# A seven-product projection: column sets reordered, pooling spread over two sets, weight sums in two slots, and the first block's sums moved from GpSimd to VectorE

## The reference

```python
h = rms_norm(x, norm_pre) * (1.0 + scale) + shift
u = h @ w_in                       # 1024 x 3720
q, k, v, f_logit, z_rwkv, p_pool, g = split(u)
y = concat[fox_attention(q, k, v, f_logit), rwkv7(z_rwkv), multiscale_pool(p_pool)] * silu(g)
x = x + gate * rms_norm(y @ w_out, norm_post)
```

## Time and profile before

| what | us |
|---|---|
| median of 3 runs (lowest, highest) | 3746.25 (3742.59, 3747.57) |
| the profiled execution | 3759.72 |
| its span, first to last instruction | 3758.0 |
| end of the projection's last product | 1525.88 |
| first product of the projection | 175.40 |
| `single` of the second block pair starts | 571.80 |
| ... of the third, of the fourth | 890.45, 1209.50 |

### The profile page before, as it was taken

How to read it: one execution, slowest core, us unless ns; L and a number is a source line. 1 busy time by engine, 2 the same in 40 slices (tenths; PEclk the granted TensorE clock), 3 DMA queues, 4 the chain that set the end, 5 groups by cost and what they waited for, 6 DMA issues and landing times. The chain is left out here.

```text
span 3758.0 us, 90231 instructions
## 1 busy us (share of the span) xinstructions
PE 3356.4 (89%) x31941; PEld 2300.8 (61%) x31941; DVE 2344.9 (62%) x4080; ACT 2051.6 (55%) x3774; POOL 1918.5 (51%) x2320
## 2 busy tenths in 40 slices
PE   6466898999899899599999789999999999989998
PEld 6322495487369349488888656656656656654454
DVE  4545452353245233578777199988989989974544
ACT  1334553454354342467776457777777767763333
POOL 1776433131332310235554269889889888871222
PEclk9688899999999999789998589999999999999999
DMA  8256552444345344323221130211202202214555
GB/s 315 73 202 213 206 178 99 155 153 144 121 149 184 113 151 158 84 67 84 70 64 43 27 84 8 55 33 30 57 15 48 56 10 53 57 49 162 192 179 184
DMA packets 237659, 406.35 MB, mean 108 GB/s; under 512 B 86542, under 2 KB 188645, under 8 KB 222085
## 3 DMA queue, kind: packets, MB, share of 16 engines
q1 hardware_dynamic: 236747, 400.56, 33.6%
q0 software_dynamic: 480, 0.14, 0.1%
HBM read 278.05 MB, written 122.59 MB: 107 GB/s over the span
## 5 line engine op out<-in xcount | busy, mean ns | idle before, releaser
L2456 ACT ACTIVATE p<-psc,xb,sc 128x512 f32<-128x512 f32 (+3 forms) x1152 | 848.3, 743 | 320.5 <-PE psc L2547 307.7
L2434 POOL TENSOR_TENSOR plo<-p 128x512 f16<-128x512 f32 (+2 forms) x864 | 903.6, 1073 | 74.3 <-ACT p L2456 72.7
L2603 DVE TENSOR_REDUCE mx<-pm 128x1 f32<-128x512 f32 (+3 forms) x1201 | 730.4, 636 | 94.0 <-PE pm L2478 80.1
L579 PE MATMUL bank<-h,ring 128*128 128x512 f16 x2688 | 625.4, 393 | 49.3 <-ACT p L719 22.7
L2526 PE MATMUL po<-v,p 128*128 128x129 f16 x4224 | 513.3, 220 | 21.4 <-POOL plo L2434 18.4
L579 PEld LDWEIGHTS bank<-h,ring 128*128 128x128 f16 x2688 | 270.9, 101 | 419.0 <-issue 95.8
L2528 PE MATMUL po<-v,plo 128*128 128x65 f16 x4224 | 483.8, 192 | 4.5 <-issue 4.5
L2526 PEld LDWEIGHTS po<-v,p 128*128 128x128 bf16 x4224 | 388.9, 97 | 124.2 <-POOL plo L2434 28.3
L584 PE MATMUL bank<-ring,h 128*128 128x128 f16 x8064 | 457.2, 219 | 2.3 <-ACT c L726 2.3
L584 PEld LDWEIGHTS bank<-ring,h 128*128 128x128 f16 x8064 | 453.7, 98 | 4.3 <-issue 2.9
L2478 PE MATMUL pm<-ka,qa 128*128 128x512 f16 (+3 forms) x1201 | 439.9, 369 | 3.3 <-DVE mx L2603 3.0
(11 more groups left out here) (385 smaller groups left out, 5777.9 us busy)
## 6 DMA issues: line engine op xcount, KB each, us to landing
ring<-scratch_ws SPq DMA_DIRECT2D x54, 1792.0 KB, 7.9
scratch_ws<-h SPq DMA_DIRECT2D x12, 1792.0 KB, 6.7
scratch_z<-stage SPq DMA_DIRECT2D x72, 256.0 KB, 7.8
y<-scratch_y SPq DMA_DIRECT2D x35, 512.0 KB
g<-scratch_g SPq DMA_DIRECT2D x35, 512.0 KB
xr<-in_x SPq DMA_DIRECT2D x34, 512.0 KB, 6.2
scratch_qk<-stage SPq DMA_DIRECT2D x64, 256.0 KB, 2.6
scratch_g<-stage SPq DMA_DIRECT2D x64, 256.0 KB, 7.9
```

Source lines behind the costliest of these rows:

```text
L579: t = nc.tensor.matmul(bank[b][:], m.ring[:, slot, l, bo, k, :], hh[:, side, r, ao, k, :], start=fresh and first, stop=last, skip_group_ch ...
L2434: nc.gpsimd.tensor_tensor(plo[:, k % NP, 0:w], p32[:, k % NP, 0:w], hi[:, 0:w], ALU.subtract)\
L2456: nc.scalar.activation(p32[:, k % NP, 0:w], psc[k % 2][:, 0:w], ACT.Exp, bias=xb[:, u, b, x // 4:x // 4 + 1], scale=m.sc[:, 0:1]).then_inc ...
L2603: nc.vector.tensor_reduce(mx[:, s, t, q:q + 1], pm[g][:, 0, 0:w], AX.X, ALU.max).then_inc(pm_d.sem, 1)
```

## The change

1. `m.kinds` becomes `m.sets`: a set is a pair of slices with a name for each side. The order is now g, g, g, g, v, v, qk, (z7, z0), qk, (z8, z1), qk, (z2, z3), qk, (z4, z5). Each pooling slice is paired with an ordinary z slice. Each raw set is fetched by two DMAs of 128 columns, where there was one of 256.
2. The first block pair's units: the row scaling of groups 1 to 3 moves from DVE in `prepare` (line 280, six instructions) to POOL in `project`; all four A parts come from ACT (two instructions), the sums S1 to S4 are on DVE (`first_sums`), and units use four slots (two of `h7`, two in `c`). The products of `single` for a group of 128 rows follow the transposes of the next group.
3. POOL does, beside the six scalings, the sums of the single slice and of set 0, and their rounding, which was ACT's. Set 1 is made in the loop.
4. Sets 1 to 13 are made at steps 1, 6, 13, 17, 21 and from 25 on every fourth step (`MADE`). `wt` has a second slot, in `xt`. ACT's and DVE's shares are done in two parts each, two steps apart (`weights_high_a`, `_b`, `weights_low_a`, `_b`). Sets 0 to 3 are made in place in the ring, where before sets 0 and 1 were.
5. The units for the second block pair begin at step 60, ten steps a group; those for the third and fourth stay at 51 and twelve.
6. p1 is gone: the first product is copied into u1, which is summed in place. The table `it16` is made in `prepare`.

```diff
-        m.kinds = (("qk", 0), ("z", 7), ("qk", 1), ("z", 0), ("qk", 2), ("z", 2), ("qk", 3), ("z", 4),
-                   ("g", 0), ("g", 1), ("g", 2), ("g", 3), ("v", 0), ("v", 1))
+        pairs = (("g", 0, 1), ("g", 2, 3), ("g", 4, 5), ("g", 6, 7), ("v", 0, 1), ("v", 2, 3), ("qk", 0, 1), ("z", 7, 0),
+                 ("qk", 2, 3), ("z", 8, 1), ("qk", 4, 5), ("z", 2, 3), ("qk", 6, 7), ("z", 4, 5))
...
+        wts = [m.wt, m.xt[:].rearrange("p s d -> p (s d)").rearrange("p (o k c) -> p o k c", o=4, k=4)]
...
-            q = 2 + 2 * (at[1] - 1) + at[2] // 4
-            return q if q < NSET else None
+        MADE = (-1, 0, 1, 6, 13, 17, 21, *range(25, 54, 4))
+        DIRECT = 4
+        def production(g, after):
+            r = g - after
+            return MADE.index(r) - 1 if 1 <= r < SUBS and r in MADE else None
+        def turns_of(sb_):
+            return (60, 10, (0, 1, 3, 4), 2, 6) if sb_ == 0 else (51, 12, (0, 2, 4, 6), 3, 7)
...
+                def first_sums(u):
+                    x = raw_slot(u)
+                    dve.wait_ge(raw_first, u + 1)
+                    tt(x[:, S1, :], x[:, A21, :], x[:, A22, :], ALU.add).then_inc(s_first, 1)
+                    tt(x[:, S3, :], x[:, A11, :], x[:, A21, :], ALU.subtract).then_inc(s_first, 1)
+                    dve.wait_ge(s_first, 4 * u + 1)
+                    tt(x[:, S2, :], x[:, S1, :], x[:, A11, :], ALU.subtract).then_inc(s_first, 1)
+                    dve.wait_ge(s_first, 4 * u + 3)
+                    tt(x[:, S4, :], x[:, A12, :], x[:, S2, :], ALU.subtract).then_inc(s_first, 1)
...
                 for u in range(18):
                     if u < 16:
-                        raw_low(u)
-                    if u == 5:
-                        weights_low(-1)
-                    if u == 11:
-                        weights_low(0)
-                    if 1 <= u < 17:
-                        low(u - 1)
-                weights_low(1)
+                        first_sums(u)
+                    if u == 6:
+                        single_low()
+                    if u >= 2:
+                        low(u - 2)
+                    if u == 14:
+                        weights_low_a(0)
+                    if u == 15:
+                        weights_low_b(0)
...
+                    if production(g, 2) is not None:
+                        weights_high_a(production(g, 2))
+                    if production(g, 4) is not None:
+                        weights_high_b(production(g, 4))
...
+                    if production(g, 3) is not None:
+                        weights_low_a(production(g, 3))
+                    if production(g, 5) is not None:
+                        weights_low_b(production(g, 5))
...
+                x_first_scaled(1)
+                single_weights()
+                x_first_scaled(2)
+                x_first_scaled(3)
+                weight_sums(0)
+                first_high()
```

More of the change, by code:

```diff
@@ L366, in kind, with item @@
         def kind(n):
-            return m.kinds[n - 1]
+            return m.sets[n - 1][0][0]
+        def item(n, side):
+            return m.sets[n - 1][side][1]
         def tile(sb_, n, half, side):
@@ L441, in unit_at @@
-        def unit_at(at):
-            if at is None or at[0] == NSB - 1:
-                return None
-            r = ended(0, at[1], at[2]) - 1 - 51
-            if r < 0 or r % 12 not in (0, 2, 4, 6) or r // 12 > 3:
-                return None
-            return (at[0] + 1) * 16 + (r // 12) * 4 + (r % 12) // 2
+        shifts = [(0, 0, 0), (0, 1, 0)] + [(n, half, side) for n in range(1, NSET + 1) if kind(n) == "z"
+                                           for half, side in ((0, 0), (1, 0), (0, 1), (1, 1)) if not is_pool(n, side)]
@@ new lines, in single @@
+                    ts = slice(j * P, (j + 1) * P)
+                    if j == 0:
+                        if sb_ == 0:
+                            pe.wait_ge(w_lo, 1)
+                        else:
+                            pe.wait_ge(c_act, sb_ * (NSET + 2))
+                            pe.wait_ge(u1_d, sb_ * NSET)
+                            pe.wait_ge(f_out, sb_)
+                    pe.wait_ge(lo_made, sb_ * 16 + 4 * (j + 1))
+                    for half, parts in enumerate((((A11, 0), (A12, 1)), ((S1, 0), (A22, 2)))):
+                        for y, (ao, bo) in enumerate(parts):
+                            for k in range(4):
+                                for x, (l, r) in enumerate(((0, 0), (0, 1), (1, 0))):
+                                    nc.tensor.matmul(bank[half][:, ts], wz[:, l, bo, k, :], hh[:, side, r, ao, k, ts],
+                                                     start=(j == 0 and y == 0 and k == 0 and x == 0),
+                                                     stop=(y == 1 and k == 3 and x == 2), skip_group_check=True)
@@ L635, in head_means @@
                     nc.tensor.matmul(pss[:], m.headmean[:], sq[:, x % 2, :], start=True, stop=True).then_inc(ss_d, 1)
-                for u in range(16):
-                    turn(u)
+                for j in range(5):
+                    if j < 4:
+                        for k in range(4):
+                            turn(4 * j + k)
+                    if j:
+                        single(0, j - 1)
                 for g in range(NG + LAST):
@@ L903, in shifted @@
                     s = t % NC
-                    dve.wait_ge(own_d, sb_ * NZ + z_order(n, half, side) + 1)
+                    dve.wait_ge(own_d, sb_ * NZ + shifts.index((n, half, side)) + 1)
                     if z_before(sb_, n, half, side):
@@ L910, in shifted @@
                         .then_inc(ready[s], 1)
-                def z_order(n, half, side):
-                    if n == 0:
-                        return half
-                    return 2 + 4 * sum(kind(y)[0] == "z" and not is_pool(y) for y in range(1, n)) + 2 * side + half
                 def z_before(sb_, n, half, side):
                     if half == 1:
-                        return sb_ * NZ + z_order(n, 0, side) + 1
-                    if sb_ == 0:
-                        return 0
-                    return (sb_ - 1) * NZ + z_order(n, 1, side) + 1
+                        return sb_ * NZ + shifts.index((n, 0, side)) + 1
+                    return (sb_ - 1) * NZ + shifts.index((n, 1, side)) + 1 if sb_ else 0
                 def value_low(sb_, n, half, side):
@@ L1076, in pieces @@
                 def pieces(sb_, n, half, side):
-                    t, x = tile(sb_, n, half, side), qk_number(sb_, n, half, side)
+                    t, x = tile(sb_, n, half, side), nth(sb_, n, half, side)
                     s = t % NC
```

492 lines of the change are left out of this document (260 added, 232 removed).

## The result

The changed kernel takes 3706.24 us (median of 4 runs, 3698.74 to 3716.05) against 3746.91 (median of 4 runs beside it): 40.7 us less, ratio 0.9893 with a 95% interval of 0.9868 to 0.9919. The forecast was 3666, 80 us less. The time lies in the stated range (3605 to 3715) but outside the forecast's own of 3640 to 3695, and about half of the gain is missing.

What follows compares the result with a forecast made beforehand. It took POOL's and DVE's turns at SBUF, not PE, to bound weight making in the first block pair. Gains 23 + 39 + 3 + 3 + 12 = 80 us gave 3680 profiled, median 3666; own range 3640 to 3695, stated range 3605 to 3715.

Steps and rivals of the forecast that it cites:

- The start: Up to the first product: it comes at 152 instead of 175.4 us, 23 us gained (18 to 42).
- Steps 1 to 57: First block pair, where 13 weight sets are made: POOL and DVE taking turns at SBUF set the length, 212 us.
- POOL and DVE together near full: Expected sign in the first block pair's steps 1 to 57, with 200 to 220 us and clock about 0.85.
- A second slot for the sums takes away POOL's wait: Weight making, first block pair: POOL's wait for the subtraction goes, but SBUF turns remain, so the slot itself gains nothing.
- Steps 58 to 98: Rest of the first block pair: products, `pss`, transposes and 15 us of waits from units among qk and pooling tiles, 145 us.
- block pairs 2 and 3: Second and third block pairs: spread pooling gains more than units among qk sets cost, 3 us gained in each.
- Back come about 9.5. Bounds are nothing and 19: Block pairs 2 and 3: new waits, 5 us at the second qk set and 4 for units between logarithms.
- The 12.5 go: Later block pairs: pairing each pooling slice with a z slice removes the 12.5 us excess behind the pooling set.
- pair 4: Fourth block pair, which has no units: 12 us gained.
- C: Rival, chance 0.14: ACT's in-order waits behind pooling tiles twice as large, production 230 us, gain 26 us, total 3720.
- D: Rival, chance 0.07: weight sets take 25 us each, results stay in PSUM, PE stands; slower, 3767 us.
- B: Rival, chance 0.18: POOL and DVE turns cost less, steps 1 to 57 take 180 us, gain 146 us, total 3600.

Runs made afterwards that it cites:

- e4: Changed kernel with the row scaling of groups 1 to 3 back on DVE in `prepare`: 3707.36 us.
- e12: Changed kernel with e7's unit places and the start of e9 (scaling on DVE, `single` products two units later): 3655.47 us, 0.9756 of the kernel before.
- e10: Changed kernel with DVE's low-half weight subtractions replaced by one-input scalings by 1.0 (low halves wrong): 3699.32 us.
- e5: Changed kernel with the order of sets turned back, qk and z first, then g and v: 3655.40 us.
- e13: Changed kernel with only one slot for the weight sums, POOL waiting for DVE's last subtraction: 3712.60 us.
- e3: e1 with both pooling slices in one set again: 3742.29 us.
- e7: Changed kernel with the units of block pairs 2 and 3 moved 44 steps earlier, same spacing (steps 7 to 49): 3666.29 us.
- e1: Changed kernel with the units of block pairs 2 and 3 at steps 8 to 44, ten steps a group: 3687.22 us, 0.9842 of the kernel before.
- e9: Changed kernel with e5's order of sets, e4's scaling on DVE, and `single` products two units later: 3649.53 us, 0.9725 of the kernel before.
- e14: e9 with the one weight-sum slot of e13: 3647.53 us, 0.9714 of the kernel before.

## Why the prediction was half right

**The start (23 forecast, 18.9 measured).** The mechanism held: sums and subtractions stretched beside POOL, and a first scaling 7 us behind the barrier. The scalings were mis-sized, 19.6 us and not 9, 3.3 each, outside the bounds of 1.2 to 1.8 that I had drawn from a cast and from half of a 2048-element instruction; the prediction's other estimate, 1.54 us, was too low as well, since the shortest of the six took 2.83. PE's order (`single` before the next transposes) was a wait that I had not counted; the scaling back on DVE brought 3.0 us (e4, 153.5), PE's order another 6.3 (e12, 147.2).

**Steps 1 to 57 (212 forecast, 198 measured).** The turns are real: e10 shows that what DVE saves in them comes off nearly in full, and e5 that qk and pooling tiles in these steps add 39 us (the prediction's sum has 29 for qk and 28 for pooling tiles at the old order). "POOL and DVE together near full" holds as well, though POOL alone is busy only 136 of 198 us and waits 51 for raw weights: DVE works in 39 of these 51, and counted instruction by instruction at least one of the two works in 182 of the 198 us. The length fell just below the 200 to 220 that I had named, and the clock was 0.92, not 0.85. "A second slot for the sums takes away POOL's wait" was right, and that nothing is gained by it as well; that it costs 8 us (e13) was not foreseen.

**Steps 58 to 98 (145 forecast, 162 measured), block pairs 2 and 3 ("Back come about 9.5. Bounds are nothing and 19").** This is the step that failed. "The 12.5 go" is right (e3: 12.8 to 15.1), and pair 4 shows it undisturbed (14.0 against 12). But what comes back is 25.6 in pair 2 and 26.1 in pair 3 (after against e5), beyond the upper bound. I had named the very chain, unit behind pooling tiles, row norm before the square, at 5 us; it took 7.5 us in two waits (710.13 and 718.99). The 4 us for units between logarithms came about as said (3.5: two waits of 2.79, where a `pss` without units waits 1.06). Two kinds I did not count: the next group's rows scaled late (2.75) and the edge from the last z set over `single` into a g set (3.7 in place of 1.3). So the waits are 15.3 and not 9.5. And I priced waits alone, putting the clock at nothing: around five of the six waits it fell to 0.50 for 3.4 or 6.8 us, and the slower matmuls made the other 10.3 of the 25.6.

Steps 58 to 98 of the first pair are the same thing, and larger. In pair 4, without units, PE takes 124.0 us for these 41 steps and stands still for 5.9 of them (first row below). In pair 2 it is 151.3 us, or 123.8 with the units moved away (e7). In the first pair it is 161.7 us and PE stands still for 30.1: 37.7 us more than in pair 4, 24.2 of them waits and 13.5 slower matmuls, where the prediction's sum has 15. The last two rows are the longest waits. The first transposes wait for scaled rows, which I had not counted, and the first `pss` behind the pooling tiles, where ACT stands 9.8 us at a unit's rounding, took 9.8 us and not 7.

```profile
1357.50:1481.50 124.00, 118.11 (x518) 52.45 (x517) 41.50 (x78) 54.91 (x72) 43.91 (x47) 1.00 0.35 124
```

```profile
370.56 1.12 PE L665 MATMUL ptr<-ident,xt 128*128 128x128 f32 x4 [7.93 <-DVE xt L909]
...
435.00 2.07 PE L673 MATMUL pss<-sq,headmean 128*128 128x512 f32 x2 [9.77 <-ACT sq L790]
```

The account up to the last product, 35.6 us short of 80: pairs 2 and 3 30.9 (forecast +6.0, measured -24.9), the start 4.1, the first pair 2.6 (14 won in its first part, 17 lost in its second), and 2.0 back in pair 4.

**Of the rivals,** C was nearest in mechanism and size: it had 160 for the last steps, a loss of 6 in pairs 2 and 3, and 3720, though its slow production (230 us) did not come. D did not come, and B's pace of the production was not reached either.

Left open: why the one slot is worth 8 us in one order of sets and 2.5, if anything, in the other; and why the last 41 steps cost 10 us more in the first pair (161.7) than in the second and third (151).

## What to carry to other kernels

A new order of work must be priced in every stretch that repeats it: this one freed the stretch in which the weights are made, which comes once, and loaded the second half of three block pairs, in which the units had stood among light sets. Two in-order chains that each hide well (running sums, the making of h) need not hide in one another; move one of them by a constant and look, before anything else is undone. Where the engine at the end is PE, add to the waits something for the clock (here 10.3 us on 15.3 us of waits), and before you buy a second buffer, find the next thing for which the same engine will wait.

## What the runs showed of the hardware

- The scaling by a column of 1024 f32 elements in SBUF takes 2.84 us on POOL and 0.68 on DVE (4.06 for six).
- POOL starts to compute some 7 us behind the barrier that ends `prepare`, whatever comes first: IOTA at 92.29 in the kernel before (barrier 85.3), the scaling at 89.09 (81.7), the product of e4 at 92.55 (85.2). Only a MEMSET did not wait: in the kernel before it ran at 85.27.
- With the two engines free to run on each other's SBUF work, the first 42 steps took 137.5 us, and 128.6 where POOL waits for DVE (e13, one execution of each).
- The granted clock around a wait of 3.7 to 3.9 us is at the lower level, 0.50, from 532.4 to 539.2 in the changed kernel (wait until 534.2), from 535.6 to 539.0 in e7 (until 535.8) and from 588.8 to 592.2 in e1 (until 589.0), and 1.00 before and after. Behind the wait of 2.79 at 786.70 it stays at 1.00 (785 to 795). e5's second pair, whose longest wait is 1.6 us, has 1.00 as a whole.
- The start's clock differs between executions of the same start: 0.68 in the changed kernel and 0.86 in e1, 0.94 in e9 and 0.70 in e14. The first product comes at nearly the same time all the same (156.5 and 155.2; 147.3 and 147.3).
- From the last product to the end, in code that is the same in all kernels, profiled executions differ by up to 30 us (2211 to 2241).
